# GpSimd splits each weight panel in pieces of 256 columns (two blocks of two layers, float32 by three matmul passes)

## The chip, the cores and the metric

The kernel runs on one core of one Trainium2 chip. The time is that of one execution on the device in microseconds, as the median of several runs. A core has TensorE (PE, matmuls; PEld is its loading of weights), VectorE (DVE), ScalarE (ACT), GpSimd (POOL) and SyncE (SP, which here only issues DMAs). Each runs its own list of instructions; they meet in semaphores.

## The reference

Two blocks of two layers each work on 1024 tokens of width 1024, all in float32. A layer normalises x, multiplies it with a wide weight matrix, runs three branches on slices of the product, and adds the sum through an output matrix:

```
h = rms_norm(x, norm_g);  proj = h @ w_in
# block 1: differential attention, short convolution, retention
merged = sum_i sigmoid(gates_i) * (branch_i @ w_branch[i]);  x = x + merged @ w_out
# block 2: 31-tap convolution of 256 channels, latent attention, spatial gating
y = concat(norm(y_conv), norm(y_mla), norm(y_sg));            x = x + y @ w_out
```

All weights pass through TensorE once per layer. The change touches only how they are made ready for it.

## The kernel before

**Panels.** The weights are cut into panels of 128 output columns. A panel of eight tiles (k) is [128, 1024] in float32, one of four tiles is [128, 512]. Each is multiplied with h in three passes that stand in for float32: the panel and h are both split in a high part (a float32 rounded to the type fp32r that TensorE takes at full rate) and a low part (the rest), and the products high x high, high x low and low x high are summed (`three_pass`, `three_pass_half`, L511 and L530). A panel over all 1024 tokens costs 48 matmuls of 512 columns; one over half of the tokens costs 24, and so does a four-tile panel over all tokens.

**Who does what.** SyncE loads panel n into `stage[:, n % 2]` once the panel two before it is split (`w_split`). GpSimd waits for the load (`w_loaded`) and for TensorE to have run the first matmul of the panel before (`panel_begun`), since `Whi` and `Wlo` have two buffers each; it writes `Whi = stage + 0` (L477, rounding to fp32r), waits for that result with `w_hi`, and writes `Wlo = stage - Whi` (L480). Then `w_split` lets TensorE begin the panel, and SyncE load the next one into the buffer. All of this is one loop over runs of panels of equal sizes, in the order in which TensorE uses them.

**Stages.** In block 1 each layer begins with attention projections, then pairs of panels with seven products for eight (here called the paired stage: ScalarE makes the high parts, L1259, and GpSimd the low ones in 512 columns, L728, function `low_products`, which the change leaves alone), then attention head by head, the branch products (panels of 512 columns, 24 matmuls), and the output projection, whose 16 panels of 1024 columns serve half of the tokens each (24 matmuls). In block 2 the input panels (48 matmuls) run beside a 31-tap convolution on VectorE (L2721, 30 steps on each of two tiles, each waiting for the one before it), then come latent attention and an output projection of eight half-token panels.

**VectorE beside GpSimd.** VectorE's instructions on the way are of two sorts: some read one tensor in SBUF and one in PSUM (L1965, `X <- psA, b_wk`), some two tensors in SBUF (L1781, `Hlo <- X, Hhi`, the low part of the next h; L2721; L1609 and L1624, sums for the paired stage).

Of the kernel before, what the change touches and what calls it, by code (L numbers as in the profile page):

```python
# [17 lines left out]
F32 = mybir.dt.float32  # L18
F32R = mybir.dt.float32r
BF16 = mybir.dt.bfloat16  # L20
ALU = mybir.AluOpType
# [9 lines left out]
P = 128  # L31
# [117 lines left out]
def taken_ahead(t):  # L149

    return sum(TAKEN[:t])
# [195 lines left out]
class C1:  # L347
# [5 lines left out]
    n = KT + 15  # L353


class C2:
# [13 lines left out]
    n = 100  # L370
# [3 lines left out]
class K:  # L374
# [8 lines left out]
    n = 512 + 1024 + 2  # L383
# [4 lines left out]
def build(nc, x, w1, par1, lamv, finalg, w2, par2, pww, sgw, sgb, consts, ropes, ng, out, xs, gs):  # L388

    with ExitStack() as top:  # L390
        def sem(name):
            return top.enter_context(nc.semaphore(name))

        def sb(name, shape, dt=F32):
            return top.enter_context(nc.sbuf_tensor(name, shape, dt))

        ident = sb("ident", [P, P])
        ones = sb("ones", [P, P])
        unseen = sb("unseen", [P, SEQ], BF16)
        with nc.sbuf_tensor("THI", [P, KT, SEQ], F32R) as THI:  # L400
            pass
        X = sb("X", [P, KT, SEQ])
        Hhi = sb("Hhi", [P, KT, SEQ], F32R)
        Hlo = sb("Hlo", [P, KT, SEQ], F32R)
        stage = sb("stage", [P, 2, KT * P])
        Whi = sb("Whi", [P, 2, KT * P], F32R)
        Wlo = sb("Wlo", [P, 2, KT * P], F32R)
        rope = sb("rope", [P, 2, SEQ])
        epsc = sb("epsc", [P, 1])
        credit = sb("credit", [P, 2])  # L410
        gg = sb("gg", [P, KT])
        sb("pad_blocks", [P, 392])
        psA = top.enter_context(nc.psum_tensor("psA", [P, 2, SEQ], F32))
        psT = top.enter_context(nc.psum_tensor("psT", [P, 2, SEQ], F32))
        env = Group()
        env.nc, env.x, env.par1, env.lamv, env.finalg, env.ng = nc, x, par1, lamv, finalg, ng
        env.par2, env.pww, env.sgw, env.sgb, env.consts = par2, pww, sgw, sgb, consts
        env.THI, env.gs = THI, gs
        env.ropes, env.out, env.xs, env.X, env.Hhi, env.Hlo = ropes, out, xs, X, Hhi, Hlo
        env.stage = stage  # L420
        env.Whi, env.Wlo, env.ident, env.ones, env.unseen = Whi, Wlo, ident, ones, unseen
        env.rope, env.epsc, env.psA, env.psT, env.sem, env.gg = rope, epsc, psA, psT, sem, gg

        s = env.s = Group()
        s.credit, s.w_split, s.w_hi, s.panel_begun = credit, sem("w_split"), sem("w_hi"), sem("panel_begun")
        s.w_loaded = [sem("w_loaded0"), sem("w_loaded1")]
        s.s_made, s.g_hi, s.g_ready = (Tally(sem(n), k * GPAIRS) for n, k in (("s_made", 4), ("g_hi", 6), ("g_ready", 6)))
        s.g_filled, s.g_sum = (Tally(sem(n), k * GPAIRS) for n, k in (("g_filled", 7), ("g_sum", 3)))
        s.g_taken = Tally(sem("g_taken"), taken_ahead(GPAIRS))
        env.out_filled, env.x_ready = Tally(sem("out_filled"), 2 * KT), Tally(sem("x_ready"), 2 * KT)  # L430
        env.saved = [Tally(sem(f"saved{half}"), 16) for half in (0, 1)]
        env.sq_done, env.sq_added = Tally(sem("sq_done"), 2 * KT), Tally(sem("sq_added"), 2 * (KT - 1))
        env.summed, env.rstd = Tally(sem("summed"), 2), Tally(sem("rstd"), 2)
        env.h_scaled, env.h_hi, env.h_lo = (Tally(sem(n), 2 * KT) for n in ("h_scaled", "h_hi", "h_lo"))
        env.par2_in = sem("par2_in")

        inputs1, tensor1, scalar1, vector1 = first_block(env)
        inputs2, tensor2, scalar2, vector2 = second_block(env)
        parts = ((w1, P1, RUNS1, 0), (w2, P2, RUNS2, BASE2))
        block = top.enter_context(nc.Block())  # L440

        @block.sync
        def _(sp):
            for (w_dram, panels, the_runs, base), inputs in zip(parts, (inputs1, inputs2)):
                inputs(sp)
                NP = len(panels)
                with sp.Fori(0, DEPTH) as L:
                    for p0, pairs, sizes, off, _seven in the_runs:
                        with sp.Fori(0, pairs) as i:
                            for b in (0, 1):  # L450

                                sp.wait_ge(s.w_split, L * NP + p0 + b + 1 + base + i * 2)
                                start = off + b * sizes[0] + i * sum(sizes)
                                sp.dma_start(stage[:, b, 0:sizes[b]], w_dram[L, :, bass.ds(start, sizes[b])])\
                                    .then_inc(s.w_loaded[b], 16)

        @block.gpsimd
        def _(pool):

            pool.memset(credit[:, 0:1], 0.0).then_inc(s.w_split, 2)  # L460
            pool.memset(credit[:, 1:2], 0.0).then_inc(s.panel_begun, 1)
            pool.wait_ge(s.w_split, 2)
            for w_dram, panels, the_runs, base in parts:
                NP = len(panels)
                with pool.Fori(0, DEPTH) as L:
                    for p0, pairs, sizes, off, seven in the_runs:
                        if seven:
                            env.low_products(pool, L, p0)
                            continue
                        with pool.Fori(0, pairs) as i:  # L470
                            for b in (0, 1):
                                n = sizes[b]
                                pool.wait_ge(s.w_loaded[b], (L * (NP // 2) + p0 // 2 + 1 + base // 2 + i) * 16)

                                pool.wait_ge(s.panel_begun, L * NP + p0 + b + 1 + base + i * 2)

                                pool.tensor_tensor(Whi[:, b, 0:n], stage[:, b, 0:n],  # L477
                                                   credit[:, 0:1].broadcast_to([P, n]), ALU.add).then_inc(s.w_hi, 1)
                                pool.wait_ge(s.w_hi, L * NP + p0 + b + 1 + base + i * 2)
                                pool.tensor_tensor(Wlo[:, b, 0:n], stage[:, b, 0:n], Whi[:, b, 0:n].bitcast(F32),  # L480
                                                   ALU.subtract).then_inc(s.w_split, 1)

        @block.tensor
        def _(pe):
            tensor1(pe)
            tensor2(pe)

        @block.scalar
        def _(act):
            scalar1(act)  # L490
            scalar2(act)

        @block.vector
        def _(dve):
            vector1(dve)
            vector2(dve)
# [2662 lines left out]
```

## Time and profile before

| | |
|---|---|
| median of 3 runs | 3559.22 us (3558.46 to 3560.29) |
| the profiled execution | 3561.47 us, its span 3559.7 us |
| TensorE busy | 98% |
| VectorE, ScalarE, GpSimd busy | 57%, 35%, 40% |
| a load of a 512 KB panel | lands 3.5 us after its issue (median of 264) |

The span runs from the first to the last instruction of the program. A row of a timeline gives the start in us from the span's beginning, the duration in us, and in brackets how long the engine was idle before it and what ended that. Ends of matmuls are modelled.

### The profile page before, as it was taken

What the parts mean: (1) busy time and instruction counts of PE and PEld (TensorE: products, weight loads), DVE (VectorE), ACT (ScalarE), POOL (GpSimd) and SP (SyncE); (2) the same over time, 40 slices, a digit from 0 to 9 for tenths busy, and PEclk for the clock granted to TensorE, in tenths of its full rate; (3) what the DMA queues carried; (4) which work ended last, traced back from release to release, by engine and by line L of the source; (5) the groups of instructions that cost most, each with busy time, mean ns of one, the idle gap of its engine ahead of it and who ended that gap; (6) DMA issues with size and microseconds to landing.
All of it is one profiled execution on the core that took longest, in us unless ns stands there. A gap on an engine that the chain in (4) does not pass through costs nothing.

```text
span 3559.7 us, 42563 instructions
## 1 busy us (share of the span) xinstructions
PE 3486.2 (98%) x15928; PEld 2706.6 (76%) x15928; DVE 2036.1 (57%) x2609; ACT 1257.3 (35%) x2177; POOL 1420.6 (40%) x766
## 2 busy tenths in 40 slices
PE   8999999999999999999999999999999999999999
PEld 7888766788878888776788877877766778776667
DVE  6432477475267522377465366974766589466653
ACT  4443244301212443244411223133556221445542
POOL 3444322253266444422244256433422455342224
PEclk9999999999999999999999999999999999999999
DMA  4223311162143232311162133211111231111112
GB/s 165 101 107 110 106 30 30 45 222 65 41 145 125 92 115 107 107 30 30 31 229 72 30 125 116 92 42 38 46 30 45 74 120 48 36 54 30 33 69 95
DMA packets 90985, 287.17 MB, mean 81 GB/s; under 512 B 9904, under 2 KB 10928, under 8 KB 90288
## 3 DMA queue, kind: packets, MB, share of 16 engines
q1 hardware_dynamic: 48960, 159.08, 14.5%
q10 hardware_dynamic: 41840, 125.52, 9.6%
q8 instruction: 129, 2.11, 0.2%
q14 instruction: 56, 0.46, 0.0%
HBM read 224.79 MB, written 59.77 MB: 80 GB/s over the span
## 4 chain that ended last, share of the span: by engine, by line
PE 87%; DVE 7%; ACT 3%; issue 1%; POOL 1%; DMA 0%; SPq 0%; ACTq 0%; POOLq 0%; DVEq 0%
PE psA L530 28%; PE psT L511 17%; PE psA L902 9%; PE psT L902 8%; PE psA L511 8%; PE psA L2194 3%; PE psT L2265 2%; PE psT L2176 2%; PE psT L864 2%; PE psA L819 1%; PE psT L803 1%; DVE b_wk L1562 1%; PE psT L2242 1%; PE psT L2171 1%; DVE b_wk L2721 1%
## 5 line engine op out<-in xcount | busy, mean ns | idle before, releaser
L477 POOL TENSOR_TENSOR Whi<-stage,credit 128x1024 fp32r<-128x1024 f32 (+1 forms) x268 | 480.7, 1794 | 1760.6 <-PE psT L511 894.7
L480 POOL TENSOR_TENSOR Wlo<-stage,Whi 128x1024 fp32r<-128x1024 f32 (+1 forms) x268 | 650.9, 2429 | 21.1
L511 PE MATMUL psT<-Hhi,Whi 128*128 128x512 f32 x1024 | 424.6, 415 | 8.6 <-DVE b_wk L1550 3.2
L511 PE MATMUL psT<-Hhi,Wlo 128*128 128x512 f32 x1024 | 404.2, 395 | 0.0
L511 PE MATMUL psT<-Hlo,Whi 128*128 128x512 f32 x1024 | 403.3, 394 | 0.0
L530 PE MATMUL psA<-Hhi,Whi 128*128 128x512 f32 x1184 | 374.9, 398 | 0.7 <-DVE b_ypad L2711 0.4
L530 PE MATMUL psA<-Hlo,Whi 128*128 128x512 f32 x1184 | 365.2, 390 | 0.0
L530 PE MATMUL psA<-Hhi,Wlo 128*128 128x512 f32 x1184 | 365.0, 389 | 0.0
L530 PEld LDWEIGHTS psA<-Hhi,Whi 128*128 128x128 f32 x1184 | 220.9, 188 | 57.0 <-issue 12.0
L728 POOL TENSOR_TENSOR Wlo<-stage,Whi 128x512 fp32r<-128x512 f32 x128 | 165.3, 1302 | 239.2 <-ACT Whi L1259 239.2
L530 PEld LDWEIGHTS psA<-Hhi,Wlo 128*128 128x128 f32 x1184 | 222.3, 188 | 46.7
L530 PEld LDWEIGHTS psA<-Hlo,Whi 128*128 128x128 f32 x1184 | 222.3, 188 | 46.4
L511 PEld LDWEIGHTS psT<-Hhi,Whi 128*128 128x128 f32 x1024 | 195.5, 191 | 59.5 <-issue 18.2
L2721 DVE SCALAR_TENSOR_TENSOR b_wk<-b_ypad,b_cur,b_wk 128x1024 f32<-128x1024 f32 x120 | 230.4, 1920 | 4.1
L511 PEld LDWEIGHTS psT<-Hhi,Wlo 128*128 128x128 f32 x1024 | 194.5, 190 | 42.7
L511 PEld LDWEIGHTS psT<-Hlo,Whi 128*128 128x128 f32 x1024 | 195.6, 191 | 39.3 <-issue 1.8
L511 PE MATMUL psA<-Hhi,Whi 128*128 128x512 f32 x480 | 193.7, 403 | 10.5 <-DVE Hlo L1781 4.4
L511 PE MATMUL psA<-Hhi,Wlo 128*128 128x512 f32 x480 | 187.9, 391 | 0.0
L511 PE MATMUL psA<-Hlo,Whi 128*128 128x512 f32 x480 | 187.8, 391 | 0.0
L1647 DVE TENSOR_TENSOR b_wk<-b_wk,psA 128x512 f32<-128x512 f32 x48 | 33.0, 688 | 214.7 <-PE psA L902 208.7
L1528 DVE CUSTOM_DVE_ANT_0 psA<-psA,unseen 128x256 f32<-128x256 f32 (+7 forms) x128 | 94.6, 780 | 102.5 <-PE psA L819 102.3
L1126 ACT ACTIVATE X<-psA,b_negmax 128x256 f32<-128x256 f32 (+7 forms) x128 | 94.1, 739 | 166.8 <-DVE b_negmax L1528 158.3
(393 smaller groups left out, 6967.4 us busy)
## 6 DMA issues: line engine op xcount, KB each, us to landing
stage<-in_w SPq DMA_DIRECT2D x264, 512.0 KB, 3.5
gs<-b_wk ACTq DMA_DIRECT2D x70, 512.0 KB, 2.7
b_wk<-gs ACTq DMA_DIRECT2D x54, 512.0 KB, 4.7
stage<-in_w SPq DMA_DIRECT2D x68, 256.0 KB, 2.7
xs<-X ACTq DMA_DIRECT2D x8, 2048.0 KB, 8.2
b_wk<-xs ACTq DMA_DIRECT2D x32, 256.0 KB, 4.3
rope<-gs ACTq DMA_DIRECT2D x14, 512.0 KB, 4.9
b_wk<-xs ACTq DMA_DIRECT2D x14, 512.0 KB, 4.5
```

Of the source, the lines that this page charges most:

```text
L477: pool.tensor_tensor(Whi[:, b, 0:n], stage[:, b, 0:n], credit[:, 0:1].broadcast_to([P, n]), ALU.add).then_inc(s.w_hi, 1)
L480: pool.tensor_tensor(Wlo[:, b, 0:n], stage[:, b, 0:n], Whi[:, b, 0:n].bitcast(F32), ALU.subtract).then_inc(s.w_split, 1)
L511: mm = pe.matmul(dst[0:M], w[:, cols], r[k][:, c], start=k == 0 and w is whi and r is rhi, stop=k == nk - 1 and end)
L530: mm = pe.matmul(dst[h], w[:, cols], r[k][:, h * HALF:(h + 1) * HALF], start=first and k == order[0] and r is rhi and w is whi, stop=last ...
L728: low = pool.tensor_tensor(slot(env.Wlo, N), product_source(n), slot(env.Whi, N).bitcast(F32), ALU.subtract)
L864: mm = pe.matmul(psAV[:, c0:], AVAL[h % 2][:, k * P:(k + 1) * P], WT[:, k, c0:], start=k == 0, stop=k == 4 * g + 3)
L902: mm = pe.matmul(dst, w[:, kc], rhs, start=begin and n in (0, 1, 3), stop=end and k == KT // 2 - 1, skip_group_check=n in (2, 4, 5, 6))
L1126: act.activation(PR[q % 2][c][:, 0:n], psA[:, A.buf(use), 0:n], ACT.Exp, bias=negmax[:, q % 2, c:c + 1], scale=-1.0, accum_out=rowsum[:, q ...
L1528: dve.tensor_tensor_reduce(out=s_neg, in0=s_neg, in1=unseen[:, SEQ - n:], scale=1.0, scalar=3e38, op0=ALU.add, op1=ALU.min, accum_out=negm ...
L2176: mm = pe.transpose(dst[:, i * P:(i + 1) * P], src[:, i * P:(i + 1) * P], ident[:])
L2194: mm = pe.matmul(dst[:, k0:k1], Q[sd][:, q * P:n], keys[g][:, 0:k1 - k0], start=True, stop=True)
L2721: ins = dve.scalar_tensor_tensor(out=YC[:, t], in0=ypad[:, t, k:k + SEQ], scalar=col(C2.conv_w + 2 * k + t), in1=YC[:, t], op0=ALU.mult, o ...
```

## The change

Both splitting instructions are issued in pieces of 256 columns: four additions and four subtractions for a panel of 1024 columns, two and two for one of 512. Only the last piece of each kind carries the signal, so GpSimd's own wait for `w_hi`, SyncE's and TensorE's for `w_split` are as they were. `PIECE = 256`.

```
-pool.tensor_tensor(Whi[:, b, 0:n], stage[:, b, 0:n],
-                   credit[:, 0:1].broadcast_to([P, n]), ALU.add).then_inc(s.w_hi, 1)
+for a in range(0, n, PIECE):
+    e = min(a + PIECE, n)
+    high = pool.tensor_tensor(Whi[:, b, a:e], stage[:, b, a:e],
+                              credit[:, 0:1].broadcast_to([P, e - a]), ALU.add)
+high.then_inc(s.w_hi, 1)
 pool.wait_ge(s.w_hi, L * NP + p0 + b + 1 + base + i * 2)
-pool.tensor_tensor(Wlo[:, b, 0:n], stage[:, b, 0:n], Whi[:, b, 0:n].bitcast(F32),
-                   ALU.subtract).then_inc(s.w_split, 1)
+for a in range(0, n, PIECE):
+    e = min(a + PIECE, n)
+    low = pool.tensor_tensor(Wlo[:, b, a:e], stage[:, b, a:e],
+                             Whi[:, b, a:e].bitcast(F32), ALU.subtract)
+low.then_inc(s.w_split, 1)
```

## Rows read from the trace of the kernel before

**Rows 1.** The page: span, and busy time of each engine.
```profile
span 3559.7 us, 42563 instructions
...
PE 3486.2 (98%) x15928; PEld 2706.6 (76%) x15928; DVE 2036.1 (57%) x2609; ACT 1257.3 (35%) x2177; POOL 1420.6 (40%) x766
```

**Rows 2.** TensorE's waits: us in total, times, longest us.
```profile
PE psA L511 <- DVE Hlo L1781: 4.4, 2, 2.2
...
PE psT L511 <- POOL Wlo L480: 3.1, 1, 3.1
```

**Rows 3.** GpSimd's groups by shape: count, busy us, mean ns, idle before.
```profile
L477 POOL TENSOR_TENSOR Whi<-stage,credit 128x1024 fp32r<-128x1024 f32 x200 | 402.0, 2010 | 1417.1 <-PE psT L511 761.8 <-PE psA L530 473.8 <-PE psA L511 150.1
...
L477 POOL TENSOR_TENSOR Whi<-stage,credit 128x512 fp32r<-128x512 f32 x68 | 78.7, 1157 | 343.5 <-PE psA L530 193.6 <-PE psT L511 132.9 <-PE psT L530 17.0
```

**Rows 4.** Timeline of GpSimd, output projection of block 1.
```profile
1048.88 1.89 POOL L477 TENSOR_TENSOR Whi<-stage,credit 128x1024 fp32r<-128x1024 f32 x1 [1.07 <-PE psA L511]
1050.85 2.40 POOL L480 TENSOR_TENSOR Wlo<-stage,Whi 128x1024 fp32r<-128x1024 f32 x1
1054.32 1.89 POOL L477 TENSOR_TENSOR Whi<-stage,credit 128x1024 fp32r<-128x1024 f32 x1 [1.07 <-PE psA L511]
```

**Rows 5.** Timeline of TensorE there: the first matmul of that panel.
```profile
1053.85 0.39 PE L511 MATMUL psA<-Hhi,Whi 128*128 128x512 f32 x1
```

**Rows 6.** L477 in the four output stages: stretch, length, busy us (count), clock, DMA.
```profile
1037.00:1114.00 77.00, 26.50 (x14) 1.00 0.51 163
2118.00:2196.00 78.00, 26.50 (x14) 1.00 0.41 125
2838.00:2878.00 40.00, 13.25 (x7) 1.00 0.49 157
3512.00:3529.00 17.00, 5.68 (x3) 1.00 0.33 93
```

**Rows 7.** Timeline where TensorE waits for a split.
```profile
1135.83 2.72 POOL L480 TENSOR_TENSOR Wlo<-stage,Whi 128x1024 fp32r<-128x1024 f32 x1
...
1138.60 0.50 PE L511 MATMUL psT<-Hhi,Whi 128*128 128x512 f32 x1
...
1139.18 1.89 POOL L477 TENSOR_TENSOR Whi<-stage,credit 128x1024 fp32r<-128x1024 f32 x1 [0.64 <-PE psT L511]
```

**Rows 8.** Timeline of GpSimd: 512 columns, two subtractions together and one addition alone.
```profile
120.35 2.55 POOL L728 TENSOR_TENSOR Wlo<-stage,Whi 128x512 fp32r<-128x512 f32 x2 [4.50 <-ACT Whi L1259]
...
707.18 1.04 POOL L477 TENSOR_TENSOR Whi<-stage,credit 128x512 fp32r<-128x512 f32 x1 [15.04 <-PE psA L530]
```

**Rows 9.** Timelines: two ready subtractions on GpSimd, and VectorE beside them.
```profile
96.47 3.00 POOL L728 TENSOR_TENSOR Wlo<-stage,Whi 128x512 fp32r<-128x512 f32 x2 [7.59 <-ACT Whi L1259]
...
96.50 1.81 DVE L1624 TENSOR_TENSOR stage<-stage 128x512 f32<-128x512 f32 x1
...
108.31 3.27 POOL L728 TENSOR_TENSOR Wlo<-b_upad,Whi 128x512 fp32r<-128x512 f32 x2 [8.85 <-ACT Whi L1259]
...
107.38 3.25 DVE L1609 TENSOR_TENSOR b_Blo<-b_wk,THI 128x1024 fp32r<-128x1024 f32 x2
```

**Rows 10.** The convolution: VectorE, GpSimd, and L477 by stretch as in rows 6.
```profile
2258.79 32.98 DVE L2721 SCALAR_TENSOR_TENSOR b_wk<-b_ypad,b_cur,b_wk 128x1024 f32<-128x1024 f32 x17
...
2273.35 3.25 POOL L480 TENSOR_TENSOR Wlo<-stage,Whi 128x1024 fp32r<-128x1024 f32 x1
...
2237.00:2356.00 119.00, 25.34 (x11) 1.00 0.18 57
```

**Rows 11.** The page's groups: the convolution's steps.
```profile
L2721 DVE SCALAR_TENSOR_TENSOR b_wk<-b_ypad,b_cur,b_wk 128x1024 f32<-128x1024 f32 x120 | 230.4, 1920 | 4.1
```

**Rows 12.** Timeline of VectorE beside rows 4.
```profile
1051.12 2.68 DVE L1781 TENSOR_TENSOR Hlo<-X,Hhi 128x512 fp32r<-128x512 f32 x1 [1.22 <-ACT Hhi L1482]
```

**Rows 13.** Timeline of GpSimd: the longest split of a 512-column panel.
```profile
805.16 1.45 POOL L477 TENSOR_TENSOR Whi<-stage,credit 128x512 fp32r<-128x512 f32 x1 [2.06 <-PE psA L530]
806.69 2.16 POOL L480 TENSOR_TENSOR Wlo<-stage,Whi 128x512 fp32r<-128x512 f32 x1
```

More of the change, by code:

```diff
@@ L455, in _ @@
                                     .then_inc(s.w_loaded[b], 16)
+        PIECE = 256
         @block.gpsimd
```

## The prediction

> **What bounds the kernel now.** The page comes first: TensorE is busy for 3486.2 of 3559.7 us and GpSimd for 40% of the span [rows 1]. On the average GpSimd has time to spare, so I looked for places where TensorE stands still for it. TensorE's list of waits shows hardly any: 3.1 us for the first panel's subtraction, and a few tenths elsewhere [rows 2]. A wait that isn't there yet can still be near. So the next views were GpSimd's groups by shape, and then its timeline in each stage, to read how long before TensorE needs a panel its split is done.
>
> The groups give the work: 200 panels of 1024 columns and 68 of 512, each with an addition (Whi) and a subtraction (Wlo) [rows 3]. Undisturbed, a 1024-column panel takes 1.89 + 0.08 + 2.40 = 4.37 us from the start of the addition to the end of the subtraction [rows 4]. GpSimd may not begin panel k+1 before TensorE has run its first matmul of panel k, so the split has one panel's matmuls to hide behind: 48 matmuls (10.9 us) in most stages, but only 24 (5.44 us) in the output projections, where a panel serves half of the tokens. There GpSimd's additions start 5.44 us apart, at 1048.88 and 1054.32, the subtraction ends at 1053.25, and TensorE begins the panel at 1053.85 [rows 4, 5]: 0.60 us later. Where TensorE does wait, it starts 0.05 us after the subtraction's end (1138.55 to 1138.60), and GpSimd's next addition starts 0.58 us after that [rows 7]. So the shortest cycle of a split is its length + 0.63 us, now 5.00 against 5.44: 0.44 us are free per panel, no more.
>
> How many panels stand so? In the four output stretches there are 14 + 14 + 7 + 3 = 38 panels [rows 6]; 34 of them have the same spacing, and three single panels elsewhere too (at 56, 2221 and 2895 us): 37. Another 13 end less than 0.3 us before TensorE begins, or are waited for: six at about 0.05 us (the first panel of all, and those such as the one subtracted at 1135.83 [rows 7]), seven at 0.13 to 0.29 us. All others have over 0.9 us.
>
> **The change, part by part.** Nothing is removed. A 1024-column panel gets 8 instructions for 2, a 512-column one 4 for 2: six more and two more. Data, order, waits and signals stay, so no piece can be used early. SyncE's next load waits for the last subtraction, 0.87 us later than now; it lands 3.5 us after its issue (the table above), while its buffer is wanted a whole cycle later, 5.9 us or more, so it stays hidden.
>
> *Price of one more instruction.* The trace has no 256-column piece. The nearest rows are the 512-column subtractions of the paired stage: two back to back take 2.55 us together, where one of 1024 takes 2.40 [rows 8, 4]: 0.15 us for one more. Bounds: the addition's two lengths, 1.04 and 1.89 us [rows 8, 4], leave 1.04 - 0.85 = 0.19 us that doesn't depend on columns, the most if nothing of it overlaps; the least is nothing, since no row excludes that queued pieces hide each other's starts. I take 0.145: 6 x 0.145 = 0.87 us on a large panel, 0.29 on a small one.
>
> The Trainium skill (GPSIMD Engine Reference, Instruction dispatch) says that a core of GpSimd starts its share of the next instruction as soon as it has finished its share of this one. By that rule, if it hid the start of every piece, the 27 us that the pieces alone cost below would fall away and the sum be 21 us; the row of two subtractions shows 0.15 us left over [rows 8], and I keep to the row.
>
> *Output stages.* A split of 4.37 + 0.87 = 5.24 us has a cycle of 5.87; less 5.44 that is 0.43 us per panel: 37 x 0.43 = 15.9 us. For the six that TensorE waits for at once all of 0.87 counts: 5.2 us. For the seven others some 0.78: 5.5 us. The small panels of the branch products have the same 5.44 us; the longest of their splits takes 3.69 (805.16 to 808.85) [rows 13], with a cycle of 4.32, so 0.29 is covered by the 5.44 us of TensorE's matmuls; uncovered it would be 68 x 0.29 = 20 us.
>
> *VectorE between the pieces.* This is the part that the diff doesn't show. A VectorE instruction that reads two tensors in SBUF and a GpSimd instruction of this kind don't run at once. A 512-column low part (Hlo<-X,Hhi) that is issued at 1051.12, while GpSimd subtracts until 1053.25, ends at 1053.80 [rows 12, 4]: it stood still for 2.13 us and then ran for 0.55. And VectorE gets in between two GpSimd instructions even when the second one is ready: two subtractions take 3.00 us with a 512-column VectorE instruction pending and 3.27 with a 1024-column one, against 2.55 [rows 9, 8]: +0.45 and +0.72 to 0.80. Now a panel has one such gap in it, after the change seven.
>
> In the convolution of block 2, VectorE does nothing else than such instructions (17 in 32.98 us in one row) [rows 10]. There the subtraction takes 3.25 us on every panel, 0.85 over its own 2.40, and the additions are 0.41 over 1.89 on average (25.34 us for 11) [rows 10]. With eight pieces and VectorE always waiting: 4.37 + 0.87 + 0.41 + 7 x 0.80 = 11.25 us, a cycle of 11.9 against 10.88: 1.0 us per panel. VectorE then does some 8.5 instructions per panel where it now does about 5.6 (10.88 / 1.94), so the 60 of a layer [rows 11] and two like them are done in 7.3 panels: 2 x 7.3 x 1.0 = 15 us. Bounds: nothing, if queued pieces keep VectorE out; and 1.1 us per gap, VectorE's whole instruction, with 0.19 per piece: a cycle of 14.3, so 3.4 us per panel and 50 us in all.
>
> The Trainium skill (SBUF — State Buffer, Who interferes with whom) calls this an exclusive lock, held for the whole instruction, in which the loser fully blocks. By its letter each gap would cost VectorE's whole instruction of 1.1 us: 3.1 us per panel and 45 us in the convolution, 3637 in all; the trace shows 0.8 [rows 9], as if GpSimd's start ran beside it.
>
> In the first half of block 1's output stages one low part per panel falls into the split: 12 panels x 0.45 = 5.4 us. Elsewhere VectorE is dense around the first panels of block 1 and the latents of block 2; six panels x 0.5 = 3 us, a guess from the sums above. The other side: VectorE gets its turn sooner. Of TensorE's waits only 4.4 us are for such an instruction (Hlo, L1781) [rows 2]; I count 2 us back, since TensorE would then wait for GpSimd there. Where VectorE isn't what TensorE waits for, its gain is worth nothing.
>
> **Sum.** 15.9 + 5.2 + 5.5 + 15 + 5.4 + 3 - 2 = 48 us. The profiled execution took 3561.5 us (span 3559.7 and 1.8 around it); 3561.5 + 48 = 3609.5. The runs' median lies 2.3 us lower: 3607 us.
>
> **Rivals.**
> 1. *GpSimd keeps its port through queued pieces.* VectorE isn't let in, and only 15.9 + 5.2 + 5.5 = 27 us remain: 3586 us. Against it: VectorE came in between two ready subtractions [rows 9]. For it: those two each had a wait of their own in front, the new pieces have none.
> 2. *Each gap is dearer*, 0.19 us per piece and a whole VectorE instruction per turn. Output stages 37 x 0.70 + 13 x 1.1 = 40, convolution 50, low parts 8, less 2 and plus 5 for the rest: 101 us, 3660; half way to it 3635. For it: small pieces are beyond what any row shows.
> 3. *No change.* If a piece costs less than 0.44 / 6 = 0.07 us and VectorE's turns fit into the spare time, TensorE never waits: 3559 us.
> 4. *Faster.* VectorE's two-input instructions now wait up to 2 us for a subtraction, then for a piece of 0.6 to 0.75 us. If TensorE's 4.4 us of waits for Hlo [rows 2] go and nothing is paid: 3559 - 4 = 3555 us. It decides only below the same 0.07 us per piece, and with a turn of VectorE in the convolution under about 0.7 us (4.37 + 0.41 + 7 x 0.7 = 9.7, within 10.25 = 10.88 - 0.63). The rows are at twice that price and just above that turn [rows 8, 9].
>
> **Numbers.** Forecast 0.55, rival 1 0.18, rival 2 0.17, rival 3 0.06, rival 4 0.04. What a measurement of this kernel tells from no change is about 0.2%, 7 us. Slower has the first three, 0.90; same 0.06; faster 0.04. The range takes in rival 1 and the nearer half of rival 2: 3580 to 3645 us.
>
> **What would show it.** Right: in the output stages additions of successive panels start some 5.87 us apart instead of 5.44, and TensorE's waits for Wlo grow from 4 to over 30 us; in the convolution panels are 11.9 us apart with about seven pieces stretched by 0.8 us, VectorE's L2721 has a mean near 1.4 us instead of 1.92 [rows 11] and the convolution ends after eight panels. The small panels show no wait, the paired stage is unchanged. Wrong in the piece's price: pieces of 256 columns follow each other at other distances than 0.57 us (additions) and 0.68 us (subtractions). Wrong in the gaps: the split in the convolution takes 6 to 7 us (rival 1) or over 13 (rival 2). The prediction falls as a whole if the spacing in the output stages stays at 5.44 us.

## The result and the profile after

The changed kernel takes 3608.9 us (median of 4 runs, 3608.4 to 3610.2) against 3559.1: 1.0142 times as long, interval 1.013 to 1.0154. The forecast was 3607 us and slower. Its profiled execution took 3608.43 us. The granted clock has no part in the 50 us: over the runs its mean is 0.994 in both kernels. The kernel with attention panels in pieces of 128 columns had one execution far above the rest (19971 us), which its time below leaves out.

The page of the changed kernel: span, busy times, and the chain that ended last; then the groups that answer to [rows 1, 3, 11]. In the changed kernel the lines stand eight later: the addition is L481, the subtraction L487, the matmuls L519 and L538, the convolution's step L2729.

```profile
span 3606.6 us, 43899 instructions
...
PE 3501.9 (97%) x15928; PEld 2702.2 (75%) x15928; DVE 1829.6 (51%) x2609; ACT 1257.0 (35%) x2177; POOL 1846.0 (51%) x2102
...
PE 80%; POOL 13%; issue 2%; ACT 2%; DVE 2%; DMA 1%; POOLq 0%; SPq 0%; ACTq 0%; DVEq 0%
...
L481 POOL TENSOR_TENSOR Whi<-stage,credit 128x256 fp32r<-128x256 f32 x936 | 694.7, 771 | 1393.1 <-PE psT L519 766.8
L487 POOL TENSOR_TENSOR Wlo<-stage,Whi 128x256 fp32r<-128x256 f32 x936 | 862.4, 950 | 21.0
...
L736 POOL TENSOR_TENSOR Wlo<-stage,Whi 128x512 fp32r<-128x512 f32 x128 | 165.3, 1302 | 229.6 <-ACT Whi L1267 229.6
...
L2729 DVE SCALAR_TENSOR_TENSOR b_wk<-b_ypad,b_cur,b_wk 128x1024 f32<-128x1024 f32 x120 | 188.2, 1569 | 4.1
```

GpSimd is still busy for only half of the span, yet it now holds 13% of the chain. VectorE is busy for 206 us less: it stands still less often beside GpSimd. Both are averages; TensorE's list of waits, which answers to [rows 2], says what it costs (waited for: us in total, times, longest):

```profile
PE psA L538 <- POOL Wlo L487: 23.1, 17, 2.3
PE psA L519 <- POOL Wlo L487: 14.5, 22, 1.8
PE psT L519 <- POOL Wlo L487: 10.6, 4, 4.9
```

48.2 us in 43 waits for the subtraction, where the kernel before had 3.4 in 3 (3.1 of them in [rows 2]). In return TensorE waits less for VectorE: over the whole list 14.9 us in 20 waits instead of 29.8 in 38, and the wait for Hlo of 4.4 us in [rows 2] is gone.

Two stages answer to the two large terms of the sum. First an output stretch of block 1 in which VectorE leaves GpSimd alone, and one addition of an earlier stretch with a low part beside it (both answer to [rows 4]):

```profile
1091.80 2.32 POOL L481 TENSOR_TENSOR Whi<-stage,credit 128x256 fp32r<-128x256 f32 x4 [1.07 <-PE psA L519]
1094.20 2.83 POOL L487 TENSOR_TENSOR Wlo<-stage,Whi 128x256 fp32r<-128x256 f32 x4
1097.66 2.33 POOL L481 TENSOR_TENSOR Whi<-stage,credit 128x256 fp32r<-128x256 f32 x4 [0.64 <-PE psA L519]
...
1054.40 2.77 POOL L481 TENSOR_TENSOR Whi<-stage,credit 128x256 fp32r<-128x256 f32 x4 [0.64 <-PE psA L519]
1057.25 2.81 POOL L487 TENSOR_TENSOR Wlo<-stage,Whi 128x256 fp32r<-128x256 f32 x4
1060.70 0.61 POOL L481 TENSOR_TENSOR Whi<-stage,credit 128x256 fp32r<-128x256 f32 x1 [0.64 <-PE psA L519]
```

Four pieces of an addition take 2.32 us where one instruction took 1.89, four of a subtraction 2.83 instead of 2.40 [rows 4]: 0.143 us for each further piece. Panels follow each other at 5.86 us (1091.80 to 1097.66), and at 6.30 where a low part falls into the split.

Then the convolution, GpSimd and VectorE (these answer to [rows 10]):

```profile
2295.19 5.58 POOL L481 TENSOR_TENSOR Whi<-stage,credit 128x256 fp32r<-128x256 f32 x4 [0.64 <-PE psA L538]
2300.85 6.09 POOL L487 TENSOR_TENSOR Wlo<-stage,Whi 128x256 fp32r<-128x256 f32 x4
2307.58 5.58 POOL L481 TENSOR_TENSOR Whi<-stage,credit 128x256 fp32r<-128x256 f32 x4 [0.64 <-PE psA L538]
2313.24 6.62 POOL L487 TENSOR_TENSOR Wlo<-stage,Whi 128x256 fp32r<-128x256 f32 x4
...
2301.36 17.92 DVE L2729 SCALAR_TENSOR_TENSOR b_wk<-b_ypad,b_cur,b_wk 128x1024 f32<-128x1024 f32 x11
```

A split takes 11.75 us from 2295.19 to 2306.94 and 12.28 for the next one, against 5.23 in the quiet stretch. The 6.52 and 7.05 us more, over seven places between eight pieces, are 0.93 and 1.01 us each time that VectorE comes in. It comes in between every two pieces: its steps start 1.63 us apart (17.92 / 11), pieces and steps by turns. Two steps of the kernel before, while GpSimd was idle (its addition at 2259.57 had 5.68 us of idle time before it, [rows 10]), show the length of a step alone:

```profile
2255.01 2.60 DVE L2721 SCALAR_TENSOR_TENSOR b_wk<-b_ypad,b_cur,b_wk 128x1024 f32<-128x1024 f32 x2
```

That is 1.30 us from start to start; the shortest of the 120 steps took 1.27 to 1.28 us.

Last the ledger, worked out from the starts of the additions in both traces: by how many us a stage became longer in each of a block's two layers. A stage runs from its first addition to that of the next one; only the output projections of block 2 are counted from their third panel, since the first two are split while attention still runs. (Counted from the first, they have +2.6 and +2.2, and latent attention -4.8 and -4.2.) It sums to the 47.0 us between the two spans.

```
stage                                   layer 1   layer 2    forecast
first panels, block 1                     +3.2      +0.4  }
branch products and gates, block 1        +1.5      +1.3  }
retention and last gates, block 1         +0.5      +0.5  }
output projections, block 1              +10.3      +8.8  }    35.0
latents to first head panels, block 2     +2.2      +2.2  }
output projections, block 2               +1.7      +1.3  }
  together                                    +33.8
convolution                              +14.3     +13.7       15
attention, block 1                        -3.9      -3.6  }    -2
latent attention, block 2                 -4.0      -3.4  }
```

### The profile page after: what moved, and what is told of

Read it like the earlier page. It is cut to its first block, busy times and chain, and to the rows that moved or that the text cites. A ratio compares the mean times of both kernels' runs of the same rounds, so it can differ in the third digit from the quotient of the medians.

```text
span 3606.6 us, 43899 instructions
## 1 busy us (share of the span) xinstructions
PE 3501.9 (97%) x15928; PEld 2702.2 (75%) x15928; DVE 1829.6 (51%) x2609; ACT 1257.0 (35%) x2177; POOL 1846.0 (51%) x2102
## 4 chain that ended last, share of the span: by engine, by line
PE 80%; POOL 13%; issue 2%; ACT 2%; DVE 2%; DMA 1%; POOLq 0%; SPq 0%; ACTq 0%; DVEq 0%
PE psA L538 23%; PE psT L519 19%; PE psA L910 8%; PE psT L910 8%; POOL Wlo L487 6%; POOL Whi L481 6%; PE psA L2202 3%; PE psA L519 3%; PE psA L827 2%; PE psT L2273 2%; PE psT L872 2%; PE psT L2184 2%; PE psT L811 1%; PE psT L2250 1%; PE psT L2247 1%
## 5 line engine op out<-in xcount | busy, mean ns | idle before, releaser
L481 POOL TENSOR_TENSOR Whi<-stage,credit 128x256 fp32r<-128x256 f32 x936 | 694.7, 771 | 1393.1 <-PE psT L519 766.8
L487 POOL TENSOR_TENSOR Wlo<-stage,Whi 128x256 fp32r<-128x256 f32 x936 | 862.4, 950 | 21.0
L519 PE MATMUL psT<-Hhi,Whi 128*128 128x512 f32 x1024 | 423.2, 413 | 14.1 <-POOL Wlo L487 10.6
L519 PE MATMUL psT<-Hhi,Wlo 128*128 128x512 f32 x1024 | 402.9, 393 | 0.0
L519 PE MATMUL psT<-Hlo,Whi 128*128 128x512 f32 x1024 | 402.3, 393 | 0.0
L538 PE MATMUL psA<-Hhi,Whi 128*128 128x512 f32 x1184 | 378.2, 401 | 23.5 <-POOL Wlo L487 23.1
L538 PE MATMUL psA<-Hlo,Whi 128*128 128x512 f32 x1184 | 366.9, 391 | 0.0
L538 PE MATMUL psA<-Hhi,Wlo 128*128 128x512 f32 x1184 | 366.1, 390 | 0.0
L538 PEld LDWEIGHTS psA<-Hhi,Whi 128*128 128x128 f32 x1184 | 220.1, 188 | 86.5 <-POOL Wlo L487 32.8
L736 POOL TENSOR_TENSOR Wlo<-stage,Whi 128x512 fp32r<-128x512 f32 x128 | 165.3, 1302 | 229.6 <-ACT Whi L1267 229.6
L538 PEld LDWEIGHTS psA<-Hhi,Wlo 128*128 128x128 f32 x1184 | 223.4, 189 | 47.2
L538 PEld LDWEIGHTS psA<-Hlo,Whi 128*128 128x128 f32 x1184 | 222.9, 188 | 47.2
L519 PEld LDWEIGHTS psT<-Hhi,Whi 128*128 128x128 f32 x1024 | 194.7, 190 | 65.7 <-issue 14.9
L519 PEld LDWEIGHTS psT<-Hhi,Wlo 128*128 128x128 f32 x1024 | 194.0, 189 | 42.5
L519 PEld LDWEIGHTS psT<-Hlo,Whi 128*128 128x128 f32 x1024 | 194.7, 190 | 38.7 <-issue 1.2
L519 PE MATMUL psA<-Hhi,Whi 128*128 128x512 f32 x480 | 198.1, 413 | 22.3 <-POOL Wlo L487 14.5
L2729 DVE SCALAR_TENSOR_TENSOR b_wk<-b_ypad,b_cur,b_wk 128x1024 f32<-128x1024 f32 x120 | 188.2, 1569 | 4.1
L519 PE MATMUL psA<-Hlo,Whi 128*128 128x512 f32 x480 | 189.0, 394 | 0.0
L519 PE MATMUL psA<-Hhi,Wlo 128*128 128x512 f32 x480 | 188.7, 393 | 0.0
```

Source lines behind the costliest of these rows:

```text
L481: high = pool.tensor_tensor(Whi[:, b, a:e], stage[:, b, a:e], credit[:, 0:1].broadcast_to([P, e - a]), ALU.add)
L487: low = pool.tensor_tensor(Wlo[:, b, a:e], stage[:, b, a:e], Whi[:, b, a:e].bitcast(F32), ALU.subtract)
L519: mm = pe.matmul(dst[0:M], w[:, cols], r[k][:, c], start=k == 0 and w is whi and r is rhi, stop=k == nk - 1 and end)
L538: mm = pe.matmul(dst[h], w[:, cols], r[k][:, h * HALF:(h + 1) * HALF], start=first and k == order[0] and r is rhi and w is whi, stop=last ...
L736: low = pool.tensor_tensor(slot(env.Wlo, N), product_source(n), slot(env.Whi, N).bitcast(F32), ALU.subtract)
L2729: ins = dve.scalar_tensor_tensor(out=YC[:, t], in0=ypad[:, t, k:k + SEQ], scalar=col(C2.conv_w + 2 * k + t), in1=YC[:, t], op0=ALU.mult, o ...
```

## The experiments

In the kernels that change only some panels, the size of a piece comes from the panel's name. The edit is the same in all of them but for the rule:

```
+def piece_of(name):
+    return 256 if RULE else KT * P          # KT * P: the whole panel
...
-if out and out[-1][2] == sizes and out[-1][4] == seven:
+if out and out[-1][2] == sizes and out[-1][4] == seven and out[-1][5] == piece:
...
-        PIECE = 256
-                    for p0, pairs, sizes, off, seven in the_runs:
+                    for p0, pairs, sizes, off, seven, PIECE in the_runs:
```

The kernel before took 3560.0 us beside the first four, 3558.4 beside the next four and 3558.7 beside the last three; each ratio is against its own.

**Pieces only where the convolution runs.**

```
RULE: name[0] in ('g', 'a', 'u', 'zs', 'v', 'zc')     # block 2's twelve input panels beside the convolution
```

> Pieces of 256 columns only for the twelve input panels of block 2 that run beside the convolution (g, a, u, zs, v, zc); all other panels whole. Theory (VectorE takes a turn between pieces, and each turn costs a whole VectorE instruction, 1.0 us): in the changed kernel the starts of GpSimd's additions fall back by 14.1 and 13.3 us over these panels, so 3559 + 27 = 3586 us. If the forecast's 0.8 us per turn were right and something else had made the stage late: 3559 + 15 = 3574 us. Rival (queued pieces keep VectorE out): no more than 3560 us.

Measured: 3586.7 us, ratio 1.0075 (1.006 to 1.0091), 26.7 us more. The two stages became 14.0 and 13.8 us longer, as in the changed kernel: the convolution's 28 us need nothing of the rest.

**Pieces only in the output projections.**

```
RULE: name[0] in ('out', 'p')
```

> Pieces of 256 columns only in the output projections (16 panels per layer of block 1, 8 per layer of block 2). Theory (the split's shortest cycle, length + 0.63 us, passes TensorE's 5.44 us): 0.42 us per panel where VectorE stays out, 0.75 to 0.87 where a low part comes in between: the ledger of the changed kernel gives 10.6 + 8.8 + 3.0 + 2.2 = 24.6, so 3583 to 3584 us. Rival (the stage is late for another reason, such as the loads): the sum over the parts doesn't hold, and this part alone gives under 10 us.

Measured: 3581.7 us, 1.0059 (1.0044 to 1.0075), 21.7 us more. The four stages: +9.7, +7.5, +1.7, +1.3, together 20.2. This is the price of the pieces alone, plus the low parts.

**Pieces only in the attention stages.**

```
RULE: name[0] in ('aq', 'ak', 'az', 'av', 'qkv', 'o')  (without the first three panels of a layer)
      or name in EARLY.values()
```

> Pieces of 256 columns only for the panels that are split during attention (aq, ak, az, av, cx 0 and 1, cb 0 and 1 of block 1 after the first three panels; qkv and o of block 2). Theory (VectorE's two-input instructions lie on the way of attention there and wait less for GpSimd; the split has 8 us or more to spare): faster, by the 4.5 + 3.8 + 4.9 + 4.5 = 17 to 18 us that the changed kernel's ledger gives back in these stages: 3541 to 3543 us. Rival (the gain there is only time regained from stalls before, since attention is bound by something else): 3559 us, no change.

Measured: 3548.9 us, 0.997 (0.9959 to 0.9981): faster than before, but 6 to 8 us short of what was expected. The ledger shows most of it: the attention stages gave -3.9, -3.2, -4.6 and -3.7, and the first two head panels of block 2, which had 0.26 us to spare, cost 2.2 us in each layer.

**The changed kernel with the convolution's steps halved.** Each VectorE step is issued as two of 512 columns.

```
-ins = dve.scalar_tensor_tensor(out=YC[:, t], in0=ypad[:, t, k:k + SEQ], ..., in1=YC[:, t], ...)
+for c0 in (0, HALF):
+    ins = dve.scalar_tensor_tensor(out=YC[:, t, c0:c0 + HALF],
+                                   in0=ypad[:, t, k + c0:k + c0 + HALF], ...,
+                                   in1=YC[:, t, c0:c0 + HALF], ...)
```

> The changed kernel (256 columns everywhere) with each step of the convolution issued on VectorE as two instructions of 512 columns. Theory (a turn costs the length of VectorE's instruction): the turn falls from 1.0 to 0.5 us, a split beside the convolution from 12.3 to about 5.2 + 7 x 0.5 + 0.2 = 8.9 us, below the 10.25 us that TensorE leaves; TensorE doesn't wait there and 27 us come back: 3609 - 27 = 3582 us. Rival (the pieces are long there for a reason of GpSimd's own, a fixed cost at each handover): splits stay near 12 us and the time near 3609.

Measured: 3581.1 us, 1.0062 (1.0047 to 1.0077): 28 us less than the changed kernel. GpSimd in the convolution of this kernel:

```profile
2277.42 4.16 POOL L481 TENSOR_TENSOR Whi<-stage,credit 128x256 fp32r<-128x256 f32 x4 [3.17 <-PE psA L538]
2281.66 4.51 POOL L487 TENSOR_TENSOR Wlo<-stage,Whi 128x256 fp32r<-128x256 f32 x4
2288.34 4.14 POOL L481 TENSOR_TENSOR Whi<-stage,credit 128x256 fp32r<-128x256 f32 x4 [2.18 <-PE psA L538]
```

A split takes 8.75 us, so a turn costs (8.75 - 5.23) / 7 = 0.50 us instead of 0.97, and GpSimd waits 2.2 us for TensorE again. The convolution stages are +0.7 and +0.4 us. A half step alone takes 0.74 us (the shortest in this trace), a whole one 1.28: the price of a turn goes with the length of VectorE's instruction, at some 0.3 us less, and it is what the convolution paid.

**The control: the kernel before with the same halved steps.**

> Control for the halved steps: the kernel before, panels whole, with each step of the convolution as two VectorE instructions of 512 columns. Theory: TensorE waits for nothing in this stage in either form, so 3559 us; with it the halved steps' gain in the changed kernel (28 us) is that of the shorter turns alone. Rival (the halved steps are better by themselves): 3559 less a good part of 28 us.

Missed: 3579.4 us, 1.0057 (1.0042 to 1.0073), 21 us slower, where no change was expected. In this kernel's page and list of waits:

```profile
L2722 DVE SCALAR_TENSOR_TENSOR b_wk<-b_ypad,b_cur,b_wk 128x512 f32<-128x512 f32 x240 | 250.6, 1085 | 4.1
...
PE psT L2171 <- DVE b_wk L2917: 12.0, 2, 6.8
```

Beside whole splits a half step has a mean of 1.09 us, so a step takes 2.17 instead of 1.92 us [rows 11]: 15 us more in each layer, and now the convolution's result comes late. TensorE waits 12 us for it, and the stages are 11.0 and 9.1 us longer. Most of the rest is the clock: beside each of the two waits it stood at its lower level for a while (a mean of 0.57 from 2362 to 2370 us, 3.4 us of full-speed work, and as much from 3040 to 3056), which the kernel before has in neither stage. In the kernel with both edits a half step takes 1.01 us. So the 28 us that halved steps gave there are not a gain of their own: they help only where pieces let VectorE in often.

**Pieces of 512 columns everywhere.**

```
-        PIECE = 256
+        PIECE = 512
```

> Pieces of 512 columns everywhere: two additions and two subtractions for a large panel, the small panels whole. Theory (0.145 us per further piece against 0.44 us of free time; 1.0 us per turn of VectorE): the output panels' 0.29 us is covered where VectorE stays out; beside the convolution a split takes 4.37 + 0.29 + 0.41 + 3 x 1.0 = 8.1 us, under the 10.25 that are free; the 12 panels with a low part and the 13 that had under 0.3 us pay some 0.3 us each, 7 us in all; attention gives back about half of what 256 columns do, 8 us: 3558 us, 3553 to 3562. Rival (every cut costs something in every stage): a third of the changed kernel's 50 us, 3575.

Measured: 3550.0 us, 0.9976 (0.9967 to 0.9986), 8 us better than expected. Two rows of the quiet output stretch:

```profile
1092.31 2.04 POOL L481 TENSOR_TENSOR Whi<-stage,credit 128x512 fp32r<-128x512 f32 x2 [0.79 <-PE psA L519]
1094.43 2.54 POOL L487 TENSOR_TENSOR Wlo<-stage,Whi 128x512 fp32r<-128x512 f32 x2
```

A split of 2.04 + 0.08 + 2.54 = 4.66 us fits under 5.44 with 0.15 to spare, the convolution's two stages cost -0.8 and 0.0, and the attention stages gave -3.8, -3.4, -3.0 and -3.9. I had expected half of the attention's gain from pieces of 512 columns: nearly all of it is there.

**Pieces of 128 columns everywhere.** PIECE = 128.

> Pieces of 128 columns everywhere: 16 instructions for a large panel, 8 for a small one. Theory: 14 x 0.145 = 2.03 us per large panel, so 1.6 us for each of 37 output panels, 2 us for 13 others, 85 in all with the low parts; beside the convolution 15 turns: a cycle of 4.4 + 2.0 + 0.4 + 15 + 0.6 = 22.4 us against 10.88, in which VectorE does 16.5 steps, so 3.8 panels x 11.5 = 44 us per layer, 87 in all; attention gives 15 back, the branch products pay 10: 3559 + 170 = 3730 us. If a turn cost the forecast's 0.8 us: 19.4 us, 3.8 x 8.5 x 2 = 65 there, 3705. Rival (the cost of a cut doesn't grow with their number, only the first one or two count): near 3610.

Measured: 3774.5 us, 1.0604 (1.0588 to 1.062), 44 us more than expected. The convolution stages: +37.9 and +45.1, 83 us where 87 were expected. The output stages: 30.7 + 27.0 + 7.9 + 5.3. Most of the miss is in the small stages: the first panels of block 1 +12.9, branch products and gates +12.7 and +11.1 where 10 had been given to both, latents +8.9 twice. GpSimd in a quiet stretch and in the convolution:

```profile
1150.46 2.90 POOL L481 TENSOR_TENSOR Whi<-stage,credit 128x128 fp32r<-128x128 f32 x8 [0.63 <-PE psA L519]
1153.44 3.37 POOL L487 TENSOR_TENSOR Wlo<-stage,Whi 128x128 fp32r<-128x128 f32 x8
1157.44 2.90 POOL L481 TENSOR_TENSOR Whi<-stage,credit 128x128 fp32r<-128x128 f32 x8 [0.64 <-PE psA L519]
...
2360.70 9.79 POOL L481 TENSOR_TENSOR Whi<-stage,credit 128x128 fp32r<-128x128 f32 x8 [0.93 <-PE psA L538]
2370.57 10.56 POOL L487 TENSOR_TENSOR Wlo<-stage,Whi 128x128 fp32r<-128x128 f32 x8
```

Fourteen more pieces add (2.90 - 1.89) + (3.37 - 2.40) = 1.98 us: 0.141 each, so the price per piece is the same at 128 as at 256 columns. In the convolution the split takes 20.43 us; (20.43 - 6.35) / 15 = 0.94 us per turn. A turn does not get cheaper when GpSimd's piece gets smaller.

The clock has a part in this one. Its mean was 0.981 in all four runs, against 0.994 to 0.995 in the kernel before: (1 - 0.981) x 3772 = 72 us of full-speed work lost instead of 19. Where TensorE waits for GpSimd anyway a slower matmul costs nothing, so up to 53 of the 216 us are the clock's; how much of the 44 us of the miss, these runs don't show.

**The attention stages again, without the two head panels that cost 2.2 us.**

```
RULE: as above, and name[0] == 'qkv' only if name not in (('qkv', 0, 0), ('qkv', 1, 0))
```

> Pieces of 256 columns for the attention panels alone, and the first two qkv panels of each layer of block 2 whole again: with them in pieces, TensorE waited 2.2 us more for the second one in each layer, since VectorE is dense there and that panel had 0.26 us to spare. Theory: 4.4 us less than with all attention panels in pieces: 3549 - 4.4 = 3544 to 3545 us. Rival (something later takes the 2.2 us back): 3549.

Measured: 3540.4 us, 0.9951 (0.9938 to 0.9965): 18 us faster than the kernel before, 4 more than expected. The two +2.2 are gone. The granted clock, on average 0.996 here and 0.9951 in the kernel with all attention panels in pieces, accounts for some 3 of the 4 us ((1 - clock) x span is 14.2 and 17.2 us).

**The output projections with the addition alone in pieces**, the subtraction whole.

```
RULE: name[0] in ('out', 'p'), and for the subtraction
-for a in range(0, n, PIECE):
-    e = min(a + PIECE, n)
+for a in (0,):
+    e = n
```

> Output projections only, and there only the addition in four pieces; the subtraction is whole. Theory (0.147 us per further piece, 0.44 us of free time per panel): the quiet panels' splits take 4.81 us, a cycle of 5.44: just covered, 0 instead of 0.42 us each. The 12 panels with a low part pay about 0.45, since VectorE now comes in before the subtraction, and the few with less to spare 2 us in all: 3559 + 7 = 3566 us, against 3582 with both in pieces. Rival (the output stages pay in proportion to the number of instructions): half of 22 us, 3570, with 0.2 us on every quiet panel.

Measured: 3563.7 us, 1.0015 (1.0007 to 1.0024), 5 us more, 2 less than expected. The quiet stretch:

```profile
1092.12 2.33 POOL L484 TENSOR_TENSOR Whi<-stage,credit 128x256 fp32r<-128x256 f32 x4 [0.69 <-PE psA L522]
1094.53 2.40 POOL L490 TENSOR_TENSOR Wlo<-stage,Whi 128x1024 fp32r<-128x1024 f32 x1
1097.60 2.33 POOL L484 TENSOR_TENSOR Whi<-stage,credit 128x256 fp32r<-128x256 f32 x4 [0.67 <-PE psA L522]
```

Three more pieces use up the 0.44 us that were free: 5.48 us between panels, where six more made it 5.86. Each quiet panel is 0.02 to 0.04 us late: the cost goes with the number of pieces beyond the cover. Where the 5 us come from is less clear than I expected. The first layer's stage is 5.6 us longer and the second's 1.3 shorter; about 1.7 us of either are the clock, which stood at its lower level for a while in one kernel and not in the other (0.83 from 1040 to 1050 us here, 1.00 before; 1.00 from 2108 to 2118 here, 0.83 before). Panels with a low part beside them are up to 0.4 us late in the first layer and not in the second.

**The attention stages with pieces of 128 columns.** The same rule, 128 for 256.

> As the version with attention's panels in pieces of 256 columns (less the first two qkv panels), but of 128. Theory (the gain is TensorE's waits for VectorE, and these are gone with 256): no further gain, 3540 us, as the ledger of 128 columns everywhere also has 3.2 us per layer of block 1 as with 256. Rival (the gain grows as VectorE's waits get shorter): 3536 or less.

Measured: 3541.4 us, 0.9949 (0.9936 to 0.9963). No further gain, as expected.

**The attention stages and the retention's panels**, the latter (rv, rz) in pieces of 512.

```
 def piece_of(name):
+    if name[0] in ('rv', 'rz'):
+        return 512
```

> The best version so far (attention's panels in pieces of 256, less the first two qkv panels) with the eight retention panels of each layer (rv, rz) in pieces of 512. By the ledger of 512 everywhere these give 0.95 and 0.4 us: 3539 us, not to be told from 3540 in the times, only in the trace. Rival (the 0.95 was time regained from a stall before it, as the branch products' panels were whole there too): nothing in the ledger either.

Measured: 3539.2 us, 0.9944 (0.9931 to 0.9958), the fastest kernel here, though its lead of 1 us on the one without the retention is within what these runs can tell; the retention stages gave 0.9 us each in the trace.

## Why the prediction came out right, point by point

**The time.** 48 us were forecast, 49.8 measured (3608.9 against 3559.1). This closeness is luck: two terms were wrong by 10 to 13 us each, in opposite directions.

**The price of a piece: right.** 0.145 us forecast; 0.143 at 256 columns, 0.141 at 128, from rows on either side of the change. The two back-to-back subtractions [rows 8] were the right neighbour, and the 0.19 us from the addition's two lengths was too much.

**Output stages, waited-for and near panels, low parts and small panels: right.** 15.9 + 5.2 + 5.5 + 5.4 + 3 = 35.0 forecast, 33.8 in the ledger; the cycle 5.86 for 5.87 forecast, and a low part adds 0.44 for 0.45. The pieces used up 0.44 us of cover, and the rest came out at full price on every panel. The kernels with pieces in the output projections alone (six more instructions: +21.7 us) and in their additions alone (three more: +5 us) show where the spare time ends. The small panels were said to show no wait; branch products and gates became 1.5 and 1.3 us longer, so a little of it was not covered.

**The convolution: mechanism right, size wrong.** The failing step is "4.37 + 0.87 + 0.41 + 7 x 0.80 = 11.25 us". VectorE does come in at each of the seven places, but a turn costs 0.93 to 1.01 us, not 0.80, and with it the split is 11.75 to 12.28 us. The cycle is 12.4 us (2295.19 to 2307.58) and 12.6 on average, where 11.9 was forecast: against TensorE's 10.88 that is 1.75 us per panel instead of 1.0, and over eight panels a layer instead of 7.3, 28 us instead of 15. The rows already had a dearer turn than 0.80: the subtraction beside the convolution's own steps took 3.25 instead of 2.40 us, 0.85 [rows 10]; the 0.72 to 0.80 came from other VectorE instructions [rows 9]. Each of those rows had one turn between two instructions with a wait of their own, while here the next piece is ready at once; that this makes the rest of the difference is an argument, and no run takes the two apart. L2729's mean of 1.57 us is a step of 1.28 and 0.3 us beside a piece of GpSimd; 1.4 had been forecast. The forecast's upper bound also had a wrong length: it took VectorE's whole instruction as 1.1 us, and a step alone takes 1.28. The Trainium skill (SBUF — State Buffer, Who interferes with whom) calls contention for the shared ports an exclusive lock, and says of VectorE's two-port modes that it is held for the whole instruction; by that letter a turn would cost 1.28 us, an estimate from the page's rule and this trace's step. This trace shows 0.97, so the truth lies between that rule and my 0.80. The halved steps (0.50 us per turn) and the pieces of 128 columns (0.94 us per turn) confirm that it is VectorE's length that counts and not GpSimd's.

**VectorE's gain: far too small.** The failing step is "Of TensorE's waits only 4.4 us are for such an instruction", and with it "I count 2 us back". TensorE's list in the kernel before has 29.8 us in 38 waits for VectorE. 3.7 of them are for L1541, which reads two tensors in SBUF, and its first line, 6.2 us, is for a TENSOR_SCALAR (L2856), which stands still beside GpSimd too. The attention stages gave 14.8 us in the ledger; by the medians the gain is 12 (33.8 + 28.0 - 49.8). In block 1 it can be named. VectorE in one attention stage (window 410 to 706), before and after, line by line (count, busy us, mean ns):

```profile
L1541 DVE SCALAR_TENSOR_TENSOR X<-X,b_inv 128x128 f32<-128x128 f32 (+7 forms) x32 | 31.4, 981 | 1.1
L1538 DVE TENSOR_SCALAR X<-X,b_inv,b_lam 128x128 f32<-128x128 f32 (+7 forms) x32 | 27.9, 872 | 1.2
L1562 DVE TENSOR_TENSOR b_wk<-b_wk,b_upad 128x512 f32<-128x512 f32 x12 | 18.7, 1558 | 0.4
```

```profile
L1549 DVE SCALAR_TENSOR_TENSOR X<-X,b_inv 128x128 f32<-128x128 f32 (+7 forms) x32 | 27.9, 871 | 1.1
L1546 DVE TENSOR_SCALAR X<-X,b_inv,b_lam 128x128 f32<-128x128 f32 (+7 forms) x32 | 21.8, 681 | 1.2
L1570 DVE TENSOR_TENSOR b_wk<-b_wk,b_upad 128x512 f32<-128x512 f32 x12 | 9.8, 815 | 0.4
```

And TensorE's waits in the same window of the kernel before:

```profile
PE psT L803 <- DVE X L1541: 1.9, 3, 0.6
PE psT L511 <- DVE b_wk L1550: 1.4, 2, 0.7
```

Both are gone from the changed kernel's window: 3.3 of the 3.9 us. They are small waits of a few tenths. In every kernel here with pieces in this stage, of 512, 256 or 128 columns, the layer's second attention part is 3.0 to 3.2 us shorter; in those without, it is unchanged to 0.05 us.

Block 2's share has two parts. Its two latent attention stages are 4.0 and 3.4 us shorter in the changed kernel, and on average 4.7 in the four kernels with pieces of 256 or 128 columns in the attention stages and hardly elsewhere. But four kernels that leave the attention's panels alone (convolution or output stages in pieces, additions alone, halved steps) show +0.9 to -3.4, -1.5 on average, in the same stages.

The first part is the wait at the head of TensorE's list in the kernel before. Here it is in that kernel, in the changed one and in the one with the attention stages alone and without the two head panels:

```profile
PE psT L2176 <- DVE b_wk L2856: 6.2, 7, 1.5
PE psT L2184 <- DVE b_wk L2864: 3.8, 3, 1.5
PE psT L2188 <- DVE b_wk L2868: 3.0, 2, 1.5
```

In the five kernels whose attention panels are whole it is 6.2 to 7.6 us, in the eight with these panels in pieces 3.0 to 4.5: some 3 us for both stages together.

The second part is the clock. It is visible in stretches of 40 us (length, PE busy, granted clock, DMA), here of the kernel before:

```profile
2520.00:2560.00 40.00, 37.55 (x173) 0.96 0.13 41
2560.00:2600.00 40.00, 39.71 (x205) 1.00 0.09 27
...
2640.00:2680.00 40.00, 38.71 (x185) 0.96 0.09 27
2680.00:2720.00 40.00, 39.96 (x199) 1.00 0.07 20
2720.00:2760.00 40.00, 36.55 (x170) 0.91 0.22 72
```

In the stretches below 1.00 TensorE stood still for 1.3 to 3.4 us, and its granted clock was at its lower level, 1.2 GHz instead of 2.4, for a short spell. A mean of 0.96 over 40 us is 0.04 x 40 = 1.6 us of full-speed work lost, 0.91 is 3.6: together 6.8 us in this stage. The changed kernel has two stretches of 0.96 there: 3.2 us, so nearly all of the 4.0 by which its stage is shorter. The kernel with the attention stages alone and without the two head panels has one:

```profile
2720.00:2760.00 40.00, 36.56 (x165) 0.96 0.36 125
```

This is 5.2 us less, of the 6.2 by which that stage is shorter. One profile of each kernel can't tell whether fewer stalls behind VectorE keep the clock up or the spells fall differently in each execution, and the unchanged stages say that about 1.5 us per stage are the latter. All executions together are firmer: the mean granted clock is 0.9945 in 16 of the kernel before and 0.996 in the five of this one; (1 - clock) x span is 19.6 and 14.2 us, 5 us less. So of its 18 us by the medians, block 1 has 7.5, the wait for L2856 3 and the clock 5; some 2 us are left. Why the clock fell less often stays open: fewer stalls behind VectorE are likely, but no run separates them from the clock.

**The rivals.** Rival 1 (GpSimd keeps its port, 27 us) is refuted: VectorE came in between every two pieces. Rival 2 was half true: the convolution shows a dearer turn, though 0.97 us and not a whole step of 1.28; its 0.19 us per piece is not shown. Rival 3 (no change) needed a piece below 0.07 us. Rival 4 (faster) named the right gain and gave it 4 us; with 12 to 15 it was one of the three largest terms, and where pieces are used only in the attention it decides the sign.

**What would have shown it.** Additions 5.87 us apart: 5.86. Waits for Wlo from 4 to over 30 us: 48. Pieces of additions 0.57 us apart: (2.32 - 0.61) / 3 = 0.57 with the single piece of 0.61 us at 1060.70. The convolution's cycle and L2721's mean: forecast 6% and 11% too low. The paired stage: unchanged, 1302 ns a product.

## What to carry to other kernels

Cutting an instruction has three prices: a fixed one per piece (here 0.14 us, paid only beyond the spare time of its cycle), most of an instruction of the other engine per gap (here 0.97 of 1.28 us) wherever that engine always has work at the shared port, and a gain wherever the other engine's results are waited for. They differ by stage, so choose the size of the piece per stage; here all of the gain came with two to four pieces, and cutting only in the attention stages turned +50 us into -17 to -20. Add up the list of waits by engine: 38 short waits behind VectorE were 30 us, a gain that no single line shows, and a total that agrees with the forecast proves none of its terms.

## What the runs showed of the hardware

- VectorE's TENSOR_SCALAR with a single tensor in SBUF stands still beside GpSimd as well. Its mean in an attention stage falls from 872 to 681 ns, and one instruction alone took 0.76 and 1.67 us in the kernel before:

```profile
712.82 0.76 DVE L1718 TENSOR_SCALAR b_wk<-b_upad,b_cur 128x1024 f32<-128x1024 f32 x1
...
725.66 1.67 DVE L1718 TENSOR_SCALAR b_wk<-b_upad,b_cur 128x1024 f32<-128x1024 f32 x1
```

  The first ran while GpSimd was idle, the second beside a subtraction (724.63 to 726.78). The Trainium skill (SBUF — State Buffer, Who interferes with whom) has tensor_scalar among the instructions that can take the shared ports; the two rows agree. My prediction had counted only instructions that read two tensors.
- VectorE gets in between two GpSimd instructions of one stream that wait for nothing, every time: eight pieces and eight VectorE instructions by turns. A queue of ready instructions keeps no port.
- A GpSimd instruction cut in n costs (n - 1) x 0.14 us, about the same at 512 (2.04 for 1.89 us), 256 (2.32) and 128 columns (2.90).
- A turn of VectorE between two pieces costs GpSimd 0.93 to 1.01 us for steps of 1.28 us alone and 0.50 us for half steps of 0.74.
- In the convolution, cutting one engine's instructions favours the other engine: GpSimd's in pieces +28 us (TensorE waits for GpSimd), VectorE's in halves +20 us (it waits for VectorE), both cut +1.2 us.
